# First phase of a fused mixer and expert kernel: shift and scale in two halves, with the input loaded first

## The chip, the core and the metric

The kernel runs as one program on one core of one Trainium2 chip. The metric is the device time of one execution in microseconds, 1215.98 us as the median of three runs (1215.55 to 1216.28). TensorE (PE in the profile) multiplies, ScalarE (ACT) and VectorE (DVE) work on tiles in SBUF and PSUM, GpSimd (POOL) does a few side operations, and SyncE (SP) issues nearly all the loads.

## The reference

One layer over 512 latent tokens of width 1024, with 256 context tokens. What the change touches is the head of the layer: six modulation vectors from the conditioning, of which the first two are shift and scale, and the normalised and modulated input h, from which every projection is made.

```python
sc = jax.nn.silu(c); scc = jax.nn.silu(c_ctx)
mod = jnp.split(sc @ w_ada[layer] + b_ada[layer], 6, axis=-1)
mod_c = jnp.split(scc @ w_ada[layer] + b_ada[layer], 6, axis=-1)
h = _modulate(_rmsnorm(x, norm1_w[layer]), mod[0][:, None], mod[1][:, None])    # h * (1 + scale) + shift
hc = _modulate(_rmsnorm(xc, norm1_w[layer]), mod_c[0], mod_c[1])
q, k, v, z, xbc, dtr, fu, su = _split_in(h @ w_in)
...    # four mixers: window attention, SSD, 2-D DFT, gated convolution
out = _merge(h, branches, w_gate, b_gate, w_branch, w_o)
x = x + mod[2] * out
h2 = _modulate(_rmsnorm(x, norm2_w[layer]), mod[3], mod[4])
x = x + mod[5] * _moe(h2, w_router, router_bias, w1, w3, w2)
return _rmsnorm(x, final_norm_w)
```

## The kernel before

Activations lie transposed: Hx holds x as 8 blocks (KD = 8) of 128 channels by 512 tokens. Each block is normalised, scaled by A1 = (1 + scale) * norm weight, and shifted. For the projections a block is split in two rounded parts, Hhi (ScalarE) and Hlo (VectorE), and a weight tile in ring_hi and ring_lo; a projection adds three products, hi by hi, hi by Hlo and lo by Hhi. The V projection instead uses the whole Hx with WV, four products of 144 columns per block, one for each 128 tokens.

The work is one list of steps, `timeline()`, written by hand. TensorE, ScalarE, VectorE and GpSimd each go through this list in its order and do their part of each step; `tile_order()` derives from it the order in which the tiles of the weight stream are loaded. An engine never overtakes in its own part. Semaphores join the engines; `full[b]` says that PSUM bank b is written, `empty[b]` that it is read.

The steps of the first phase are these. `("mr", u)`: the product of the two silu vectors with unit u of w_ada (a 512-column piece of 2048 KB; units 0 and 1 hold the shift, units 2 and 3 the scale), eight products into a PSUM bank that ScalarE copies to `modrow[u]`. `to_columns(u)`: four products of two columns each that turn that row into columns. `("ssq",)`: the sum of squares of x over the partitions, from which ScalarE's root and VectorE's reciprocal make `rsx`. `("mod", 0)`: VectorE adds the bias to shift and scale (`mods`), makes A1, and the eight blocks are modulated and split. `("csq",)`, `("ssqc",)`: the same sums for the context. `("xbc", 0)`: the first projection tile and, woven into it, the V products; `("v", c)` only carries its results. `keep_warm(n)` is n products of ones, whose result nobody reads. Modulation row and block: unit 0 gives the shift of blocks 1 to 4, unit 2 their scale, units 1 and 3 those of blocks 5 to 8.

SyncE issues the loads at the program's start in the order cols, rows, ada 0, ada 1, x, ada 2, ada 3, and then the stream of tiles, with WV behind the first one and the context behind the second.

Of the kernel before, what the change touches and what calls it, by code (L numbers as in the profile page):

```python
# [26 lines left out]
P = 128  # L27
# [159 lines left out]
def bank_plan(steps):  # L187
# [3 lines left out]
    for s in steps:  # L191
# [26 lines left out]
        elif k in ("ssq", "ssqc"):  # L218
            b = 3
        elif k in ("ynorm", "macc", "zk", "rtk", "dt", "csq"):  # L220
            continue
        elif k in ("mr", "v"):
            b = 4 + s[1]
        elif k == "z":
            b = 3 + s[1]
        elif k == "rt":
            b = 7
        elif k == "g2":
            b = 3
        elif k == "pick":  # L230
            b = s[1]
        elif k == "bexp":
            b = 5
        elif k == "up0":
            continue
        else:
            b = 7
# [54 lines left out]
def build(nc, xT, ctxT, adaw, stream, consts, cossin, dft, cols, rows, wv, wrt, umap, wa, wb, w2, h2d, ybuf, gfin, out):  # L292
# [12 lines left out]
    ada = [at(f"ada{i}", o, [P, UNIT]) for i, o in enumerate((32768, 73728, 90112, 177344))]  # L305
# [160 lines left out]
    hm_ready, h_ready, padz = map(sem, "hm_ready h_ready padz".split())  # L466
# [103 lines left out]
    def _(sp):  # L570
        sp.dma_start(QC[:, :], cols).then_inc(small_in, 16)
        sp.dma_start(RW[:, :], rows).then_inc(small_in, 16)
        sp.dma_start(ada[0][:, :], adaw[0]).then_inc(ada_in[0], 16)
        sp.dma_start(ada[1][:, :], adaw[1]).then_inc(ada_in[1], 16)
        sp.dma_start(Hx[:, :, :], xT).then_inc(x_in, 16)
        sp.dma_start(ada[2][:, :], adaw[2]).then_inc(ada_in[2], 16)
        sp.dma_start(ada[3][:, :], adaw[3]).then_inc(ada_in[3], 16)
        rings = {True: [], False: []}
        for i, x in enumerate(order):
# [22 lines left out]
            if x == ("xbc", 0):  # L602
                sp.dma_start(WV[:, :, :], wv).then_inc(wv_in, 16)
            if x == ("xbc", 1):
                sp.dma_start(hcx[:, :, :], ctxT).then_inc(c_in, 16)
# [72 lines left out]
    def _(pe):  # L678
# [65 lines left out]
        def to_columns(u):  # L744

            job_read(pe, ("mr", u))
            for j in range(4):
                o = (4 * u + j) * 2
                ins = mm(bk(0)[:, o:o + 2], modrow[:, u, j * P:j * P + P], QC[:, Q_SUM:Q_SUM + 2], True, True)
# [6 lines left out]
        def project(s, cols, x, ctx_side):  # L756
# [7 lines left out]
            return ins.then_inc(full[b], 1)  # L764

        for s in steps:
# [17 lines left out]
            elif k0 == "mr":  # L784
# [5 lines left out]
                if u > 1:  # L790
                    for q in ((0, 1), (2,))[u - 2]:
                        to_columns(q)
                    if u == 2:
                        keep_warm(8)
# [5 lines left out]
            elif k0 == "mod":  # L800
                to_columns(3).then_inc(full[0], 1)
            elif s == ("xbc", 0):

                b, hi, lo = claim(pe, s), hi_place(s), lo_place(s)
                keep_warm(3)
                for c in range(NCH):
                    claim(pe, ("v", c))
                pe.wait_ge(hi_ready, 1)
                for k in range(KD + 1):
                    if k < KD:  # L810
                        w = hi[:, k * P:k * P + P]
                        pe.wait_ge(hhi_ready, k + 1)
                        mm(bk(b), w, Hhi[:, k, :], k == 0, False)
                        pe.wait_ge(hlo_ready, k + 1)
                        mm(bk(b), w, Hlo[:, k, :], False, False)
                    if k:
                        if k == 1:
                            pe.wait_ge(wv_in, 16)
                        pe.wait_ge(h_ready, k)
                        for c in range(NCH):  # L820
                            ins = mm(bk(4 + c)[:, 0:VD], Hx[:, k - 1, c * P:c * P + P], WV[:, k - 1, :], k == 1, k == KD)
                            if k == KD:
                                ins.then_inc(full[4 + c], 1)
                pe.wait_ge(lo_ready, 1)
                for k in range(KD):
                    ins = mm(bk(b), lo[:, k * P:k * P + P], Hhi[:, k, :], False, k == KD - 1)
                ins.then_inc(full[b], 1)
# [332 lines left out]
    def _(act):  # L1160
# [16 lines left out]
        for s in steps:  # L1177
# [16 lines left out]
            elif k0 == "mr":  # L1194
                b, _n = plan[s]
                if s[1] == 2:
# [6 lines left out]
                if s[1] == 3:  # L1203
                    split_hi(0)
            elif s == ("mod", 0):

                def whole(k):
                    act.wait_ge(hlo_ready, k + 1)
                    A(Hx[:, k, :], Hx[:, k, :], ACT.Identity, bias=mods[:, k, 0:1]).then_inc(*t(h_ready))

                for k in range(KD):
                    act.wait_ge(hm_ready, k + 1)
                    A(Hhi[:, k, :], Hx[:, k, :], ACT.Identity, bias=mods[:, k, 0:1]).then_inc(*t(hhi_ready))
                    if k:
                        whole(k - 1)
                whole(KD - 1)
                split_hi(1)
            elif k0 == "csq":
                act.wait_ge(c_in, 16)
                for k in range(NCC * 2):  # L1220
                    A(sq[:, KD + k, :], hcx[:, 2 * k:2 * k + 2, :].rearrange("p a n -> p (a n)"), ACT.Square).then_inc(*t(sq_ready))
            elif k0 in ("xbc", "xbcc"):
# [223 lines left out]
    def _(v):  # L1446
# [95 lines left out]

        sum_squares(0, KD)

        for s in steps:
# [5 lines left out]
            if k0 in ("ssq", "ssqc", "ssq2"):  # L1551
# [3 lines left out]
                else:  # L1555
                    out = {"ssq": rsx, "ssqc": rsc}[k0]
                    link(V_.reciprocal(out[:, :], out[:, :]))
                    if k0 == "ssqc":
# [7 lines left out]
            elif k0 == "csq":  # L1566
                sum_squares(KD, KD + NCH)
            elif k0 == "sw":
                job_full(v, s)
                V_.tensor_copy(swv[:, :], bk(b)[:, 0:NE]).then_inc(*t(empty[b], plan[s][1]))  # L1570
            elif s == ("mod", 0):
                job_full(v, s)
                TT(mods[:, 0:16, :], bk(b)[:, 0:32].rearrange("p (j w) -> p j w", w=2),
                   hb(QC[:, Q_BADA:Q_BADA + 16], 2), ALU.add).then_inc(*t(empty[b], plan[s][1]))
# [702 lines left out]
```

## Time and profile before

| | |
|---|---|
| median of three runs | 1215.98 us |
| profiled execution | 1215.87 us |
| its span | 1214.0 us |
| TensorE busy | 1130.3 us (93%) |
| VectorE busy | 558.7 us (46%) |
| ScalarE busy | 315.0 us (26%) |
| GpSimd busy | 127.1 us (10%) |
| mean granted TensorE clock | 0.985 |
| moved by DMA | 273.87 MB, mean 226 GB/s |

The span runs from the first to the last recorded instruction, and the execution's own time is 1.9 us more. Times in the rows count from the span's start. A row of the timeline gives start, duration, engine and line, the operation with what it writes and reads, how many instructions are merged in it, and in brackets how long the engine was idle before and what it waited for. One fp32 product of TensorE stands as two instructions, so eight products appear as x16.

### The profile page before, as it was taken

The page shows a single profiled execution, that of the slowest core. Times are in us where ns is not written, and L with a number is a line of the kernel's source. Part 1 is how long each engine was busy: PE and PEld are TensorE (multiplying, and loading weights), DVE is VectorE, ACT ScalarE, POOL GpSimd, SP SyncE. Part 2 cuts the span into 40 slices and gives each one's busy share as a digit, 9 for nine tenths or more (in the row PEclk, how much of TensorE's full clock was granted, in tenths as well). Part 3 has the DMA queues.
Part 4 walks back from the last instruction along what each step waited for, and adds up shares of the span by engine and source line. Part 5 has one row for each costly group of instructions (what it writes and reads, how often), then busy time and mean ns, then how long its engine had stood idle before and what let it go on. Part 6 is the DMA issues. An engine that isn't in the chain of part 4 may idle for free.

```text
span 1214.0 us, 16058 instructions
## 1 busy us (share of the span) xinstructions
PE 1130.3 (93%) x5708; PEld 708.7 (58%) x5708; DVE 558.7 (46%) x987; ACT 315.0 (26%) x537; POOL 127.1 (10%) x180
## 2 busy tenths in 40 slices
PE   4999999999999999999999999899999999977786
PEld 2788878877666777777778787433333333322223
DVE  2777577735676776656454455421112111211114
ACT  3653312133333434323333333100000000000003
POOL 0000000000120010012000100122112222211110
PEclk8899999999999999999999998999999999999998
DMA  9422636620111111112212567899999999999965
GB/s 386 163 87 93 255 138 227 236 93 18 53 53 53 53 53 52 53 52 86 71 64 93 195 247 275 353 403 388 418 426 426 420 426 413 425 428 424 426 280 218
DMA packets 39573, 273.87 MB, mean 226 GB/s; under 512 B 7274, under 2 KB 7786, under 8 KB 27616
## 3 DMA queue, kind: packets, MB, share of 16 engines
q1 hardware_dynamic: 33920, 264.89, 54.3%
q0 software_dynamic: 5600, 8.26, 1.9%
q8 instruction: 34, 0.56, 0.2%
q14 instruction: 19, 0.16, 0.0%
HBM read 269.86 MB, written 13.37 MB: 233 GB/s over the span
## 4 chain that ended last, share of the span: by engine, by line
PE 75%; DMA 11%; DVE 8%; ACT 3%; issue 2%; SPq 1%; DVEq 0%; POOL 0%; ACTq 0%; POOLq 0%
PE psum L680 71%; DMA ering<-in_wb 9%; DMA ada<-in_adaw 2%; DVE amx L1712 1%; DVE sc L1701 1%; PE psum L696 1%; PE psum L982 1%; DMA xr<-token_rows,tabt 1%; DVE ring_lo L1456 1%; PE psum L718 1%; DVE ytmp L1456 1%; ACT ring_hi L1163 1%; ACT E L1163 0%; DVE sg L1456 0%; PE psum L1063 0%
## 5 line engine op out<-in xcount | busy, mean ns | idle before, releaser
L680 PE MATMUL psum<-ering,xs 128*64 128x512 f32 x1056 | 237.3, 600 | 27.3 <-DMA ering<-in_wb 14.4
L680 PE MATMUL psum<-Hhi,ring_hi 128*128 128x512 f32 x472 | 192.8, 408 | 2.7 <-DVE ring_lo L1456 1.7
L680 PE MATMUL psum<-Hlo,ring_hi 128*128 128x512 f32 x472 | 186.3, 395 | 0.1
L680 PE MATMUL psum<-Hhi,ring_lo 128*128 128x512 f32 x472 | 182.9, 390 | 0.0
L680 PEld LDWEIGHTS psum<-ering,xs 128*64 128x64 f32 x1056 | 72.8, 137 | 168.9 <-issue 132.3
L1456 DVE TENSOR_TENSOR ring_lo<-ring,ring_hi 128x1024 fp32r<-128x1024 f32 x83 | 102.9, 1239 | 104.6 <-ACT ring_hi L1163 103.3
L1456 DVE TENSOR_TENSOR sg<-sg,psum 128x256 f32<-128x256 f32 x66 | 27.8, 421 | 259.2 <-ACT sg L1163 258.0
L680 PE MATMUL psum<-ering,at 128*64 128x512 f32 x528 | 119.4, 597 | 0.7 <-DVE ysb L1456 0.7
L1163 ACT ACTIVATE ring_hi<-ring 128x1024 fp32r<-128x1024 f32 x83 | 88.0, 1060 | 78.3 <-DMA ring<-in_stream 49.9
L680 PEld LDWEIGHTS psum<-Hhi,ring_hi 128*128 128x128 f32 x472 | 89.2, 189 | 26.8 <-issue 8.6
L680 PEld LDWEIGHTS psum<-Hlo,ring_hi 128*128 128x128 f32 x472 | 89.1, 189 | 20.9 <-issue 2.4
L680 PEld LDWEIGHTS psum<-Hhi,ring_lo 128*128 128x128 f32 x472 | 88.5, 188 | 19.9
L1163 ACT ACTIVATE sg<-psum 128x256 f32<-128x256 f32 x33 | 12.7, 383 | 243.2 <-PE psum L680 243.1
L680 PEld LDWEIGHTS psum<-ering,at 128*64 128x64 f32 x528 | 35.5, 136 | 65.2 <-issue 65.2
L1456 DVE TENSOR_TENSOR ysb<-psum,G 128x512 f32<-128x512 f32 x33 | 22.8, 691 | 80.3 <-PE psum L680 77.0
L1163 ACT ACTIVATE gth<-psum,half 128x512 f32<-128x512 f32 x32 | 22.0, 688 | 124.2 <-PE psum L680 119.3
L1163 ACT ACTIVATE at<-psum 128x256 f32<-128x256 f32 x33 | 12.7, 383 | 141.1 <-PE psum L718 141.1
L2058 POOL TENSOR_TENSOR xdd<-xs,wdd 128x512 f32<-128x512 f32 x10 | 10.4, 1042 | 331.2 <-DVE zs L1684 241.0
L680 PE MATMUL psum<-bhi,ring_hi 128*128 128x512 f32 x96 | 40.9, 426 | 0.0
L1163 ACT ACTIVATE sc<-sc,amx 128x512 f32<-128x512 f32 (+1 forms) x32 | 24.8, 776 | 56.0 <-DVE amx L1713 56.0
L680 PE MATMUL psum<-blo,ring_hi 128*128 128x512 f32 x96 | 38.0, 395 | 0.0
L680 PE MATMUL psum<-bhi,ring_lo 128*128 128x512 f32 x96 | 38.0, 395 | 0.0
(339 smaller groups left out, 1525.8 us busy)
## 6 DMA issues: line engine op xcount, KB each, us to landing
ering<-in_w SPq DMA_DIRECT2D x28, 2048.0 KB, 16.1
ering<-in_wb SPq DMA_DIRECT2D x28, 2048.0 KB, 18.3
ering<-in_wa SPq DMA_DIRECT2D x28, 2048.0 KB, 16.6
ring<-in_stream SPq DMA_DIRECT2D x87, 512.0 KB, 4.1
ada_ring<-in_stream SPq DMA_DIRECT2D x32, 512.0 KB, 3.6
ada<-in_adaw SPq DMA_DIRECT2D x4, 2048.0 KB, 16.9
gat<-expert_rows SPq DMA_DIRECT2D x4, 1024.0 KB, 8.3
Hx<-in_xT SPq DMA_DIRECT2D x1, 2048.0 KB, 16.9
```

The lines of the kernel that those rows point to most:

```text
L680: return nc.tensor.matmul(out, lhsT, rhs, start=start, stop=stop)
L696: ins = nc.tensor.transpose(XT[h][:, q * P:q * P + P], xr[h][:, q * P:q * P + P], ID)
L718: ins = nc.tensor.transpose(AT[h][:, q * P:q * P + P], sg[h][:, q * P:q * P + P], ID)
L982: ins = nc.tensor.transpose(bk(b, 2)[:, i * P:i * P + P], sc[:, h % 3, i * P:i * P + P], ID)
L1163: return nc.scalar.activation(out, in_, f, **kw)
L1456: return V_.tensor_tensor(out, a, b, op)
L1701: ins = V_.scalar_tensor_tensor(sc[:, h % 3, 0:S], bk(3 + g), HD ** -0.5, CT[:, C_MASK + mo:C_MASK + mo + S], ALU.mult, ALU.add)
L1712: link(V_.tensor_reduce(amx[:, h, 0:1], sc[:, h % 3, 0:W], AX.X, ALU.max))
L2058: G_.tensor_tensor(xdd[:, :].rearrange("p (h n) -> p h n", h=8), xs[:, c, :].rearrange("p (h n) -> p h n", h=8), hb(wdd[:, c, d * 8:d * 8 ...
```

## The change

The list of steps is written anew at its head. Only units 0 and 2 are multiplied before `("mod", 0)`, which now makes shift, scale and A1 of blocks 1 to 4 alone. `("xa", 0)` and `("xa", 1)` hold the first four blocks' products of the first tile and of V, with `("mr", 1)` between them; `("mr", 3)` and the new `("modb",)` make the second half, and `("xbc", 0)` keeps blocks 5 to 8. The loads go out as x, ada 0, ada 2, first tile, WV, ada 1, ada 3, context. The modulation itself is rewritten: VectorE multiplies a block by rsx alone, ScalarE makes Hhi from that with A1 as scale and the shift as bias, VectorE makes the whole block with both, and subtracts Hhi for Hlo; ScalarE's second pass over Hx is gone. The sixteen warming products stand ahead of the first unit, eight before unit 2, and the three before the first tile are gone. Four of the first tile's eight lo products come before the last two-column products.

```diff
-    t = [("mr", 0), ("mr", 1), ("mr", 2), ("ssq",), ("mr", 3), ("mod", 0), ("csq",), ("xbc", 0)] + [("v", c) for c in range(NCH)]
+    t = [("mr", 0), ("ssq",), ("mr", 2), ("mod", 0), ("xa", 0), ("mr", 1), ("xa", 1), ("mr", 3), ("modb",), ("csq",), ("xbc", 0)]
+    t += [("v", c) for c in range(NCH)]
...
+        sp.dma_start(Hx[:, :, :], xT).then_inc(x_in, 16)
         sp.dma_start(ada[0][:, :], adaw[0]).then_inc(ada_in[0], 16)
-        sp.dma_start(ada[1][:, :], adaw[1]).then_inc(ada_in[1], 16)
-        sp.dma_start(Hx[:, :, :], xT).then_inc(x_in, 16)
         sp.dma_start(ada[2][:, :], adaw[2]).then_inc(ada_in[2], 16)
-        sp.dma_start(ada[3][:, :], adaw[3]).then_inc(ada_in[3], 16)
...
             if x == ("xbc", 0):
                 sp.dma_start(WV[:, :, :], wv).then_inc(wv_in, 16)
+                sp.dma_start(ada[1][:, :], adaw[1]).then_inc(ada_in[1], 16)
+                sp.dma_start(ada[3][:, :], adaw[3]).then_inc(ada_in[3], 16)
+                sp.dma_start(hcx[:, :, :], ctxT).then_inc(c_in, 16)
...                                                              (TensorE)
+        def first_blocks(k):
+            x = ("xbc", 0)
+            b, w = plan[x][0], hi_place(x)[:, k * P:k * P + P]
+            pe.wait_ge(hhi_ready, k + 1)
+            mm(bk(b), w, Hhi[:, k, :], k == 0, False)
+            pe.wait_ge(hlo_ready, k + 1)
+            mm(bk(b), w, Hlo[:, k, :], False, False)
...
+                    pe.wait_ge(x_in, 16)
+                    keep_warm(16)
+                if u == 2:
+                    to_columns(0)
+                    keep_warm(8)
+                if u == 3:
+                    claim(pe, ("modb",))
+                    to_columns(1)
...
+            elif k0 == "modb":
+                pe.wait_ge(lo_ready, 1)
+                for k in range(4):
+                    lo_block(k)
+                to_columns(3).then_inc(full[3], 1)
+            elif k0 == "xa":
...
+                for k in range(2 * s[1], 2 * s[1] + 2):
+                    first_blocks(k)
+                    if k:
+                        v_blocks(k - 1)
+                if s[1] == 1:
+                    v_blocks(3)
...                                                              (ScalarE)
+            elif k0 == "modb" or s == ("mod", 0):
+                act.wait_ge(a1_ready, 1 + (k0 == "modb"))
+                for k in range(4) if k0 == "mod" else range(4, KD):
                     act.wait_ge(hm_ready, k + 1)
-                    A(Hhi[:, k, :], Hx[:, k, :], ACT.Identity, bias=mods[:, k, 0:1]).then_inc(*t(hhi_ready))
+                    A(Hhi[:, k, :], Hx[:, k, :], ACT.Identity, scale=A1[:, k, 0:1], bias=mods[:, k, 0:1]).then_inc(*t(hhi_ready))
...                                                              (VectorE)
+        def over_root(k):
+            TT(Hx[:, k, :], Hx[:, k, :], rsx[:, :], ALU.mult).then_inc(*t(hm_ready))
...
+                for k in range(o, o + 4):
+                    if k < 3:
+                        over_root(k + 1)
                     v.wait_ge(hhi_ready, k + 1)
+                    V_.tensor_scalar(Hx[:, k, :], Hx[:, k, :], A1[:, k, 0:1], mods[:, k, 0:1], ALU.mult, ALU.add).then_inc(*t(h_ready))
+                    v.wait_ge(h_ready, k + 1)
+                    TT(Hlo[:, k, :], Hx[:, k, :], Hhi[:, k, :].bitcast(F32), ALU.subtract).then_inc(*t(hlo_ready))
+                if k0 == "mod":
+                    split_lo(0)
+                    for k in range(4, KD):
+                        over_root(k)
```

On TensorE, the program's head before the change, up to the products of block 3 (ada_54 to ada_57 are units 0 to 3, one_t the warming products, `psum<-QC,modrow` the two-column products, WV,Hx a V group):

```order
L680 MATMUL psum<-ada_54,silp 32x512 x8
L680 MATMUL psum<-ada_55,silp 32x512 x8
L680 MATMUL psum<-QC,modrow 128x2 x8
L680 MATMUL psum<-one_t 128x128 x8
L680 MATMUL psum<-ada_56,silp 32x512 x8
L680 MATMUL psum<-sq,one_t 128x512
L680 MATMUL psum<-QC,modrow 128x2 x4
L680 MATMUL psum<-ada_57,silp 32x512 x8
L680 MATMUL psum<-QC,modrow 128x2 x4
L680 MATMUL psum<-one_t 128x128 x3
L680 MATMUL psum<-Hhi,ring_hi 128x512
L680 MATMUL psum<-Hlo,ring_hi 128x512
```

The same engine in the changed kernel, from the last two-column products before the first block to those of the last unit:

```order
L683 MATMUL psum<-QC,modrow 128x2 x4
L683 MATMUL psum<-Hhi,ring_hi 128x512
L683 MATMUL psum<-Hlo,ring_hi 128x512
L683 MATMUL psum<-Hhi,ring_hi 128x512
L683 MATMUL psum<-Hlo,ring_hi 128x512
L683 MATMUL psum<-WV,Hx 128x144 x4
L683 MATMUL psum<-ada_55,silp 32x512 x8
L683 MATMUL psum<-Hhi,ring_hi 128x512
L683 MATMUL psum<-Hlo,ring_hi 128x512
L683 MATMUL psum<-WV,Hx 128x144 x4
L683 MATMUL psum<-Hhi,ring_hi 128x512
L683 MATMUL psum<-Hlo,ring_hi 128x512
L683 MATMUL psum<-WV,Hx 128x144 x8
L683 MATMUL psum<-QC,modrow 128x2 x4
L683 MATMUL psum<-ada_57,silp 32x512 x8
L683 MATMUL psum<-Hhi,ring_lo 128x512 x4
L683 MATMUL psum<-QC,modrow 128x2 x4
```

Units 1 and 3 stood ahead of every product of a block; now unit 1 has two blocks and one V group ahead of it, and unit 3 four blocks and four V groups.

On VectorE, the changed kernel from the first A1 on (before, each block had two SCALAR_TENSOR_TENSOR, one for Hx and one for Hlo):

```order
L1608 SCALAR_TENSOR_TENSOR A_116<-mods,QC 128x8
L1479 TENSOR_TENSOR Hx<-Hx,rsx 128x512
L1615 TENSOR_SCALAR Hx<-Hx,A_116,mods 128x512
L1479 TENSOR_TENSOR Hlo<-Hx,Hhi 128x512
L1479 TENSOR_TENSOR Hx<-Hx,rsx 128x512
L1615 TENSOR_SCALAR Hx<-Hx,A_116,mods 128x512
L1479 TENSOR_TENSOR Hlo<-Hx,Hhi 128x512
```

A block of the first half has three operations in a row there, one of the second half two, since its product with rsx is done before the second A1.

## Rows read from the trace of the kernel before

**Rows 1.** Chain of waits, 0 to 70 us: start, duration, what.
```profile
3.05 21.27 DMA ada<-in_adaw
...
24.37 8.26 PE psum L680 x42
...
38.70 15.20 PE psum L680 x85
```

**Rows 2.** Load issues: timeline, ada tiles' landing times, and the page's issue list.
```profile
1.64 0.42 SPq L573 DMA_DIRECT2D ada<-in_adaw  x1
...
2.58 0.43 SPq L575 DMA_DIRECT2D Hx<-in_xT  x1
...
3.60 0.76 SPq L577 DMA_DIRECT2D ada<-in_adaw  x1
...
DMA to landing us min/median/max: 8.0/16.9/25.6
...
Hx<-in_xT SPq DMA_DIRECT2D x1, 2048.0 KB, 16.9
```

**Rows 3.** Timeline of TensorE, 9 to 33 us.
```profile
9.78 3.33 PE L680 MATMUL psum<-ada,silp 128*32 128x512 f32 x16 [9.78 <-DMA ada<-in_adaw]
...
14.58 1.92 PE L680 MATMUL psum<-ada,silp 128*32 128x512 f32 x16 [1.46 <-DMA ada<-in_adaw]
...
16.43 1.95 PE L680 MATMUL psum<-QC,modrow 128*128 128x2 f32 x16
...
18.24 2.03 PE L680 MATMUL psum<-one_t 128*128 128x128 f32 x16
...
24.37 3.64 PE L680 MATMUL psum<-ada,silp 128*32 128x512 f32 x16 [4.10 <-DMA ada<-in_adaw]
...
27.94 2.01 PE L680 MATMUL psum<-sq,one_t 128*128 128x512 f32 x2
...
30.66 1.92 PE L680 MATMUL psum<-ada,silp 128*32 128x512 f32 x16
```

**Rows 4.** Timeline, 33 to 35 us: last two-column products, bias, A1.
```profile
33.37 1.05 PE L680 MATMUL psum<-QC,modrow 128*128 128x2 f32 x8 [0.78 <-ACT modrow L1163]
34.53 0.19 DVE L1456 TENSOR_TENSOR mods<-psum,QC 128x32 f32<-128x32 f32 x1 [0.34 <-PE psum L680]
34.75 0.18 DVE L1576 SCALAR_TENSOR_TENSOR A<-mods,QC 128x16 f32<-128x16 f32 x1
```

**Rows 5.** Windows of 1 us: engines' busy time, then granted clock, DMA share, GB/s.
```profile
22.00:23.00 1.00, 0.00 (x0) 0.00 (x0) 0.93 (x3) 1.00 (x3) 0.00 (x0) 0.96 1.11 475
29.00:30.00 1.00, 1.00 (x5) 0.51 (x3) 0.00 (x0) 0.00 (x0) 0.00 (x0) 0.63 1.05 422
36.00:37.00 1.00, 0.32 (x1) 0.28 (x1) 0.81 (x2) 1.00 (x2) 0.00 (x0) 0.79 1.06 438
43.00:44.00 1.00, 1.00 (x7) 0.96 (x7) 1.00 (x3) 1.00 (x3) 0.00 (x0) 0.80 0.03 12
```

**Rows 6.** Groups by form: busy us, mean ns of one, idle before.
```profile
L1456 DVE TENSOR_TENSOR sq<-sq 128x512 f32<-128x512 f32 x10 | 6.9, 692 | 16.0 <-ACT sq L1163 15.6
...
L1602 DVE TENSOR_SCALAR macc<-ada_ring,sil 128x512 f32<-128x512 f32 x8 | 3.9, 486 | 7.3 <-DMA ada_ring<-in_stream 7.1
...
L1557 DVE RECIPROCAL rsx<-rsx 128x512 f32<-128x512 f32 x1 | 3.4, 3352 | 5.0 <-ACT rsx L1163 5.0
...
L1163 ACT ACTIVATE Hhi<-Hx,mods 128x512 fp32r<-128x512 f32 x8 | 5.7, 720 | 1.6 <-DVE Hx L1579 1.6
...
L1163 ACT ACTIVATE sq<-Hx 128x512 f32<-128x512 f32 x8 | 4.3, 614 | 2.3 <-DMA Hx<-in_xT 2.3
```

**Rows 7.** Timeline of TensorE: V groups at both clocks, eight lo products.
```profile
39.29 2.12 PE L680 MATMUL psum<-WV,Hx 128*128 128x144 f32 x8
...
44.16 1.14 PE L680 MATMUL psum<-WV,Hx 128*128 128x144 f32 x8
...
51.79 2.10 PE L680 MATMUL psum<-Hhi,ring_lo 128*128 128x512 f32 x8
```

**Rows 8.** Timeline: the copy of the first tile's result, and the first context tile.
```profile
54.01 0.60 ACT L1163 ACTIVATE pads<-psum 128x512 f32<-128x512 f32 x1 [2.83 <-PE psum L680]
...
66.44 0.36 PE L680 MATMUL psum<-hchi,ring_hi 128*128 128x256 f32 x1 [0.69 <-DVE hclo L1456]
```

More of the change, by code:

```diff
@@ L217, in bank_plan @@
             b = 0
-        elif k in ("ssq", "ssqc"):
+        elif k in ("ssq", "ssqc", "modb"):
             b = 3
-        elif k in ("ynorm", "macc", "zk", "rtk", "dt", "csq"):
+        elif k == "mr" and s[1] % 2:
+            b = 1 + s[1] // 2
+        elif k in ("ynorm", "macc", "zk", "rtk", "dt", "csq", "xa"):
             continue
@@ L304, in build @@
     Hlo = at("Hlo", 177344, [P, KD, S], FR)
-    ada = [at(f"ada{i}", o, [P, UNIT]) for i, o in enumerate((32768, 73728, 90112, 177344))]
+    ada = [at(f"ada{i}", o, [P, UNIT]) for i, o in enumerate((32768, 73728, 177344, 90112))]
     modrow = at("modrow", 110784, [P, 4, S])
@@ L764, in project, with lo_block, v_blocks @@
             return ins.then_inc(full[b], 1)
+        def first_blocks(k):
[5 more added lines that the diff above has]
+            mm(bk(b), w, Hlo[:, k, :], False, False)
+        def lo_block(k):
+            x = ("xbc", 0)
+            return mm(bk(plan[x][0]), lo_place(x)[:, k * P:k * P + P], Hhi[:, k, :], False, k == KD - 1)
+        def v_blocks(k):
+            pe.wait_ge(h_ready, k + 1)
+            for c in range(NCH):
+                ins = mm(bk(4 + c)[:, 0:VD], Hx[:, k, c * P:c * P + P], WV[:, k, :], k == 0, k == KD - 1)
+                if k == KD - 1:
+                    ins.then_inc(full[4 + c], 1)
         for s in steps:
@@ L800, in _ @@
             elif k0 == "mod":
-                to_columns(3).then_inc(full[0], 1)
-            elif s == ("xbc", 0):
[L804 to L827, printed above, removed]
@@ new lines, in _ @@
+                to_columns(2).then_inc(full[0], 1)
+            elif k0 == "modb":
[4 more added lines that the diff above has]
+            elif k0 == "xa":
+                if s[1] == 0:
+                    claim(pe, ("xbc", 0))
+                    for c in range(NCH):
+                        claim(pe, ("v", c))
+                    pe.wait_ge(hi_ready, 1)
+                    pe.wait_ge(wv_in, 16)
+                for k in range(2 * s[1], 2 * s[1] + 2):
[4 more added lines that the diff above has]
+                    v_blocks(3)
+            elif s == ("xbc", 0):
+                for k in range(4, KD):
+                    first_blocks(k)
+                    if k > 4:
+                        v_blocks(k - 1)
+                v_blocks(KD - 1)
+                for k in range(4, KD):
+                    ins = lo_block(k)
+                ins.then_inc(full[plan[s][0]], 1)
@@ L1591, in _ @@
+                if k0 == "mod":
+                    split_lo(0)
+                    for k in range(4, KD):
+                        over_root(k)
             elif k0 == "macc":
```

54 lines of the change are left out of this document (18 added, 36 removed).

## Prediction

> **What bounds the kernel now.** The change touches only the first 54 us, so I read the chain of waits of that stretch first. It shows one DMA wait of 21.27 us up to 24.3 us, then TensorE for 8.26 us, and from 38.70 us TensorE again for 15.20 us, to 53.9 us [rows 1]. That last moment, when the first projection tile (xbc 0) and the V products are complete, is the yardstick below: all later work follows it. Next the DMA issues: the loads are queued one behind another, and each 2048 KB load lands about 4.9 us after the one ahead: ada 0 at 9.6 us, Hx at 19.5, the last at 29.2 (issue plus time to landing), the others evenly between [rows 2]. Unit 3 of w_ada, the second half of the scale, lands at 29.2 us, but its products start at 30.66 [rows 3]: TensorE is late for its own load by 1.5 us. A1 is ready at 34.93 us [rows 4]. Last the granted clock. It falls from full (2.4 GHz) to half (1.2 GHz) late in the slice 22 to 23 us, after TensorE has stood idle since 20.3, and again in 36 to 37 us, after a stretch with only the two-column products and the three warming products; it is back in 29 to 30 us, 5.0 us after dense work began at 24.37, and in 43 to 44 us, 6.7 us after 36.7 [rows 5]. At 9.78 us the column shows full speed, but eight products take 3.33 us there and 1.92 us later [rows 3], so the first burst runs at about half speed too.
>
> **Loads.** Hx now stands where ada 0 stood and lands at 9.6 us, ada 0 at 14.5, ada 2 at 19.5. Behind them come the ring tile and WV (512 and 576 KB, at 4.9 us for 2048 KB together 2.6 us: 22.1), ada 1 (27.0) and ada 3 (31.9), 2.7 us later than now.
>
> **Up to the first A1.** The sixteen warming products start at 9.75. Eight cost 2.03 us at full speed [rows 3], 0.254 each. The bounds are 4.1 us (full throughout, hidden before the load at 14.5) and 8.1 us (half throughout, end at 17.9). I take half speed for the first 3.3 us, as the first burst has it now: 6.5 products, the other 9.5 cost 2.4 us, end 15.45. Products of unit 0: 1.92, to 17.4; the sum product, 2.01 at half speed [rows 3], 1.0 here, to 18.4; its inputs are there (eight squares of 0.61 with additions of 0.69 behind them [rows 6], 16 us). Two-column products of unit 0: 1.0, eight warming products 2.03, to 21.4; unit 2: 1.92, to 23.3. Copy and hand-over 0.72, four two-column products 1.05 [rows 4], three small VectorE operations instead of two (0.51 plus 0.2 [rows 4]): A1 of blocks 1 to 4 at 25.8 us, 9.1 us earlier than now. The reciprocal, 3.35 us [rows 6], started at about 19.1 and is done.
>
> **First half, blocks 1 to 4.** ScalarE's Hhi has a scale read from a tensor besides the bias. A tensor bias costs 0.11 us (0.720 against 0.614 for the squares [rows 6]); no row has both operands. Between 0.72 and 0.94 I take 0.82. The Trainium skill, "ScalarE: Activation LUTs", section "What ACT_TABLE_LOAD costs", gives each such pointer operand about 93 ns; the trace's 106 for one agrees, and by the page the two places where this Hhi heads a chain cost 0.19 us together. VectorE has three operations per block instead of two: Hx times rsx (0.69), the TENSOR_SCALAR (0.49, as the macc row) and the subtraction (0.69) [rows 6], with hand-overs 1.95 us. Hlo of block 1 stands at 27.8, of 2 at 29.75, of 3 at 31.7, of 4 at 32.95. Dropping ScalarE's second pass over Hx gains nothing, ScalarE being free here.
>
> **What now stands between the scale's second half and TensorE.** TensorE takes instructions in written order. ada 1 and ada 3 wait behind products: the V group of block 1 ahead of unit 1, then blocks 3 and 4 with three more V groups, the two-column products of unit 1, and only then unit 3. From 30.0 us, at full speed: four V groups at 1.14 (4.56), units 1 and 3 (3.84), four Hhi/Hlo products at 0.23 (2.10 for eight, less the tail of the last; 0.92) [rows 7], two-column products 1.0, four lo products 0.92 (they cover the copy of unit 3's result), two-column products 1.05: 12.3 us, so 42.3. The load of ada 3, landed at 31.9, is met only near 40: it isn't the bound any more. But the clock. From 23.3 to 30.0 TensorE has four two-column products and three 512-column ones, less than before either fall now. I take the clock as half from there and back 5.0 us after 30.0 (the burst at 24.37 is dense like this one; 6.7 is the other bound). A V group takes 2.12 at half against 1.14 [rows 7], so 5.0 us at half lose 2.3. Ready at 44.6. The skill's rule against this change, "TensorE: Matmul & The Clock Gate", section "HAM oscillation — how this bites in real kernels", says in my words that each wait long enough drops the clock and makes the next burst begin slow; the rows of both falls agree. By that rule both gaps pay; by a clock that holds, neither.
>
> **Second half, blocks 5 to 8.** Small operations 0.75: A1 at 45.4. Hhi 0.82, TENSOR_SCALAR and Hlo 1.23: 47.5; each further Hlo 1.25 later (Hx times rsx was done beside the first half, by 37), so that of block 6 at 48.75. Until then TensorE has had three products since 44.6, again a gap of 4 us. From 48.8: one Hlo product 0.23, four V groups 4.56, two more blocks 0.92, four lo products 0.92: 6.6, to 55.4. The clock again costs 2.3: 57.7 us against 53.9. So +3.8 us.
>
> Nothing gives it back later. The context chain starts from this same end; at 66.44 us TensorE has been idle 0.69 us for it [rows 8], which is all that a slow start of the next tile could hide. Csq, the context squares and the splits of ring tiles 2 and 3 lie beside the V products as now. The DMA queue is idle after 43 us [rows 5], so the moved loads delay none. GpSimd's clearing of pads waits for unit 1's products and moves to about 35 us, long before the first copy into pads [rows 8]. The profiled execution took 1215.87 us (span 1214.0 plus 1.9 around it), 0.1 under the median of 1215.98: 1215.87 + 3.8 = 1219.7 us.
>
> **Rivals.**
>
> A. The clock holds. Sixteen warming products lie at the head and V products in the first gap's wake; if neither gap drops the clock both terms of 2.3 go: 53.1, and if the warming products run at full speed too, unit 0 starts 0.85 earlier: 52.3, so -1.6 us, 1214.3. It decides at xbc 0's end: not slower from 53.9 down, which needs nearly both gaps. For it: two-column and warming products kept the clock between 16.4 and 20.3. Against: both falls now followed lighter work of 3 to 4 us.
>
> B. One gap keeps the clock, or falls only after it, so that one term stays: +1.5, 1217.4.
>
> C. The warming products run at half speed throughout, end at 17.9 (+2.4), and unit 0 follows at half (3.64 against 1.92, +1.7): 1223.8. For it: no row shows what 128-column products alone do to a clock that is down. Against: the eight 512-column products restored it by 14.58.
>
> D. The products of unit 3 meet their load, as its early place in the queue suggests. From 31.9: unit 3 1.92, copy 0.72, columns 1.05, small operations 0.75, second A1 at 36.3; Hlo of block 6 3.3 us later, then 6.6 and 2.3: 48.6, so -5.3, 1210.6. For it: now unit 3 does follow its load by 1.5 us only. Against: the written order puts 8.4 us of other products between 30.0 and unit 3, so this needs my reading of who waits for whom to be wrong.
>
> **Chances.** Forecast 0.50, with its own range 1218.3 to 1222.0 (the second bound of the clock's return, 6.7 instead of 5.0 us, twice 0.8, and Hhi's price). A 0.13, B 0.17, C 0.15, D 0.05. What a measurement here can tell from no change is 0.2%, 2.4 us: the edges are 1213.5 and 1218.4. Slower: nearly all of the forecast and C, 0.64. Same: A, B and the forecast's fringe, 0.27. Faster: D and a part of A, 0.09. The range of 8 in 10 takes in A and nearly C: 1214.0 to 1223.5.
>
> **What would show it.** Right: A1 of the first half near 26 us, a granted clock that falls in 24 to 29 us and again around 45 to 49, unit 1's products after 31 us although ada 1 landed at 27, unit 3's near 40, the second A1 near 45, and pads of xbc 0 near 57.8 instead of 54.01 [rows 8]. Wrong: full clock across either gap, unit 3 before 36 us, or VectorE's blocks at another pace than 1.95 and 1.25 us. From the tile after xbc 0 on, every row should stand at one constant distance from its place now.

## The result, and the profile after

| | before | after |
|---|---|---|
| median, 7 runs of each side by side | 1215.98 us (1214.49 to 1219.37) | 1220.41 us (1219.57 to 1221.75) |
| ratio to before, 95% interval | | 1.0032 (1.0019 to 1.0045) |
| profiled execution | 1215.87 us | 1221.74 us |
| its span | 1214.0 us | 1219.9 us |
| mean granted TensorE clock | 0.985 | 0.979 |

The medians lie 4.4 us apart, and the ratio makes it 3.9 us (2.3 to 5.5); 3.8 us were forecast. One execution of before beside a later experiment took 2891.94 us and is left out of its ratio. The chain of waits of the changed kernel, 0 to 60 us (start, duration, what), answers to [rows 1]:

```profile
1.64 8.15 DMA Hx<-in_xT
...
9.92 13.82 PE psum L683 x90
...
24.48 0.90 PE psum L683 x7
25.38 0.79 issue
26.16 0.82 ACT Hhi L1193
...
30.12 14.65 PE psum L683 x89
...
45.39 0.82 ACT Hhi L1193
...
46.31 0.56 DVE Hx L1615
...
46.89 0.70 DVE Hlo L1479
...
47.64 9.35 PE psum L683 x43
```

The long load wait is gone from the chain: x, at its start, is the only load in it. In its place the chain leaves TensorE twice for several microseconds, at 25.4 and at 44.8 us, for the small operations, ScalarE and VectorE. The 14.65 us on TensorE between them are the stretch in which unit 3 is queued behind products. TensorE's timeline (start, duration, instructions merged, idle before) answers to [rows 3, 7]:

```profile
9.92 6.34 PE L683 MATMUL psum<-one_t 128*128 128x128 f32 x32 [9.92 <-DMA Hx<-in_xT]
...
16.19 1.92 PE L683 MATMUL psum<-ada,silp 128*32 128x512 f32 x16
...
24.48 1.05 PE L683 MATMUL psum<-QC,modrow 128*128 128x2 f32 x8 [0.78 <-ACT modrow L1193]
...
30.71 2.12 PE L683 MATMUL psum<-WV,Hx 128*128 128x144 f32 x8
...
32.77 3.35 PE L683 MATMUL psum<-ada,silp 128*32 128x512 f32 x16
...
36.63 1.14 PE L683 MATMUL psum<-WV,Hx 128*128 128x144 f32 x8
...
40.91 1.92 PE L683 MATMUL psum<-ada,silp 128*32 128x512 f32 x16
...
49.41 2.12 PE L683 MATMUL psum<-WV,Hx 128*128 128x144 f32 x8
```

The first V group, unit 1 and the V group at 49.41 run at half speed, the V group at 36.63 and unit 3 at full. The same in windows of one us (each engine's busy time, then granted clock, DMA share, GB/s), as in [rows 5]:

```profile
28.00:29.00 1.00, 0.67 (x2) 0.30 (x2) 1.00 (x3) 0.08 (x1) 0.00 (x0) 0.94 0.96 410
...
35.00:36.00 1.00, 1.00 (x8) 0.00 (x0) 1.00 (x2) 0.00 (x0) 0.00 (x0) 0.65 1.00 418
...
45.00:46.00 1.00, 0.00 (x0) 0.00 (x0) 0.27 (x3) 0.61 (x1) 0.00 (x0) 0.97 0.00 0
...
52.00:53.00 1.00, 1.00 (x6) 0.90 (x6) 0.97 (x2) 0.58 (x1) 0.00 (x0) 0.61 0.08 25
```

The clock falls from full (2.4 GHz) to half (1.2 GHz) at the end of 28 to 29 us and of 45 to 46 us, each time in a stretch in which TensorE mostly waits, and comes back in 35 to 36 and 52 to 53. The yardstick, against 54.01 us in [rows 8]:

```profile
57.09 0.60 ACT L1193 ACTIVATE pads<-psum 128x512 f32<-128x512 f32 x1 [4.51 <-PE psum L683]
```

### The profile page after: what moved, and what is told of

Its sections match the earlier page's. It is cut to its first block, busy times and chain, and to the rows that moved or that the text cites. A ratio compares the mean times of both kernels' runs of the same rounds, so it can differ in the third digit from the quotient of the medians.

```text
span 1219.9 us, 16117 instructions
## 1 busy us (share of the span) xinstructions
PE 1141.6 (94%) x5734; PEld 716.9 (59%) x5734; DVE 562.2 (46%) x999; ACT 310.3 (25%) x529; POOL 127.1 (10%) x180
## 4 chain that ended last, share of the span: by engine, by line
PE 76%; DMA 10%; DVE 8%; ACT 3%; issue 2%; SPq 0%; DVEq 0%; POOL 0%; ACTq 0%; POOLq 0%
PE psum L683 73%; DMA ering<-in_wb 6%; DMA ering<-in_wa 3%; DVE amx L1743 1%; DVE sc L1732 1%; PE psum L699 1%; PE psum L1012 1%; DMA xr<-token_rows,tabt 1%; DVE ring_lo L1479 1%; PE psum L721 1%; DMA Hx<-in_xT 1%; DVE ytmp L1479 1%; ACT ring_hi L1193 1%; ACT E L1193 0%; DVE sg L1479 0%
## 5 line engine op out<-in xcount | busy, mean ns | idle before, releaser
L683 PE MATMUL psum<-ering,xs 128*64 128x512 f32 x1056 | 240.7, 607 | 23.6 <-DMA ering<-in_wa 11.8
```

The lines of the kernel that those rows point to most:

```text
L683: return nc.tensor.matmul(out, lhsT, rhs, start=start, stop=stop)
```

## The experiments

The theory: the loss is the order of TensorE's work. Unit 3 waits behind products instead of for its load, and each of the two gaps costs its waiting and then time at half clock. The rivals: the gaps' clock is worth nothing; the modulation's extra VectorE work carries the loss; unit 3 is load-bound. Below, "copy" is the start of the copy into pads, after at 57.09 and before at 54.01 us. Each ratio is to runs of before on the same chip, with its 95% interval; the medians of before there were 1217.5 to 1217.6 us, not 1215.98, so the ratios say more than the medians. The copy also carries what happened before the change's order matters: the first half's two-column products (unit 2's) come at 23.6 to 24.7 us, as the head's warming products take 5.6 to 6.6 us. Where it matters, the stretch from those products to the copy is given, 57.09 - 24.48 = 32.61 us in the changed kernel (32.49 in its second profile).

**Second gap filled by order.** `e1_units_first`:

```diff
-    ("mod", 0), ("xa", 0), ("mr", 1), ("xa", 1), ("mr", 3), ("modb",), ("csq",), ("xbc", 0)]
+    ("mod", 0), ("xa", 0), ("mr", 1), ("mr", 3), ("modb",), ("xa", 1), ("csq",), ("xbc", 0)]
```

> The changed kernel with units 1 and 3 and the second A1 moved ahead of blocks 3 and 4 and their V groups (steps xa 0, mr 1, mr 3, modb, xa 1). Theory (TensorE's written order makes the second A1 late, and the gap it leaves costs the clock): A1 comes at about 42.5 us instead of 45.3, blocks 3 and 4 fill the gap of 44.8 to 47.6, the granted clock does not fall there, and the copy into pads stands at about 53.5 us instead of 57.09: about 3.5 us under the changed kernel, level with before (-0.5 to +1). Rival (the second half waits for loads or for VectorE's pace, not for TensorE's order): pads stays at 56 to 57 and the time within 1 us of the changed kernel.

Measured: 1214.20 us (7 runs), ratio 0.9963 (0.9949 to 0.9976). Its timeline:

```profile
40.80 0.95 PE L683 MATMUL psum<-QC,modrow 128*128 128x2 f32 x8
...
52.54 0.60 ACT L1193 ACTIVATE pads<-psum 128x512 f32<-128x512 f32 x1 [2.96 <-PE psum L683]
```

The copy comes 4.55 us earlier than in the changed kernel, and the stretch is 28.16 us, 4.45 less. Only two blocks' products moved: they now fill the second gap, and the granted clock stays at 1.00 through 44 to 48 us. The rival that the order behind unit 1 is indifferent is out.

**Second gap filled with warming products alone.** `e4_warm_second_gap`, in the modb step of TensorE:

```diff
                 to_columns(3).then_inc(full[3], 1)
+                keep_warm(11)
```

> The changed kernel with eleven warming products (2.8 us at full speed) behind the last two-column products, that is in the gap of 44.8 to 47.6 us. They add no wait, since Hlo of block 5 is not there before 47.6. Theory (the second gap's price is the clock, 2 to 2.5 us): the granted clock stays at 1.00 from 36 us on, pads stands at about 54.8 instead of 57.09, -2.3 us. Rival (the clock falls all the same, because such products don't count as work, or TensorE waits for VectorE's blocks anyway): pads within 0.5 us of 57.09, time unchanged.

Measured: 1216.22 us (12 runs), ratio 0.9988 (0.9977 to 0.9999). Its timeline:

```profile
24.74 1.05 PE L683 MATMUL psum<-QC,modrow 128*128 128x2 f32 x8 [0.78 <-ACT modrow L1194]
...
45.00 2.70 PE L683 MATMUL psum<-one_t 128*128 128x128 f32 x22
...
55.60 0.60 ACT L1194 ACTIVATE pads<-psum 128x512 f32<-128x512 f32 x1 [2.63 <-PE psum L683]
```

The gap's wait is still there, only its clock is kept: no fall from 37 us to the copy. From unit 2's two-column products to the copy the changed kernel takes 57.09 - 24.48 = 32.61 us, this one 30.86. So the second gap's clock alone is worth 1.75 us (1.9 if counted from the second A1 on), and the rest of what the order gave, 2.7 us, is the waiting itself.

**Both gaps.** `e5_warm_both_gaps`, in addition:

```diff
                 to_columns(2).then_inc(full[0], 1)
+                keep_warm(6)
...
                     first_blocks(k)
+                    if k == 0:
+                        keep_warm(5)
```

> The changed kernel with eleven warming products in the second gap, where they kept the clock full and brought the copy into pads from 57.09 to 55.60, and now also six behind the first half's two-column products and five behind the first Hlo product, in the gap of 25.4 to 30.1 us. Theory (the first gap costs about 2.3 us by its clock): the clock does not fall near 29 us, unit 1's products take 1.9 us instead of 3.4, pads at 53 to 53.7. Rival (such products do not keep the clock here, or they delay the first block): the fall stays, pads at 55.5 or later.

Measured: 1214.45 us (12 runs), ratio 0.9983 (0.9971 to 0.9995). Its timeline, and its windows in the two gaps:

```profile
24.12 1.05 PE L683 MATMUL psum<-QC,modrow 128*128 128x2 f32 x8 [0.78 <-ACT modrow L1197]
...
31.18 1.92 PE L683 MATMUL psum<-ada,silp 128*32 128x512 f32 x16
...
52.17 0.60 ACT L1197 ACTIVATE pads<-psum 128x512 f32<-128x512 f32 x1 [2.64 <-PE psum L683]
```

```profile
28.00:29.00 1.00, 1.00 (x8) 0.96 (x9) 0.99 (x2) 0.44 (x1) 0.00 (x0) 1.00 1.11 475
...
45.00:46.00 1.00, 0.54 (x3) 0.23 (x2) 0.97 (x2) 0.97 (x3) 0.00 (x0) 1.00 0.00 0
```

The clock is full across both, and unit 1 takes 1.92 instead of 3.35 us. The same stretch takes 52.17 - 24.12 = 28.05 us: the first gap's clock is worth 30.86 - 28.05 = 2.81 us. Both together 4.56; forecast twice 2.3. Each price rests on one profile, but the stretch itself came out within 0.12 us in the two profiles of the changed kernel.

**Unit 1 before every block.** `e2_unit1_before_blocks`:

```diff
-    ("mod", 0), ("xa", 0), ("mr", 1), ("xa", 1), ("mr", 3), ("modb",), ("csq",), ("xbc", 0)]
+    ("mod", 0), ("mr", 1), ("xa", 0), ("mr", 3), ("modb",), ("xa", 1), ("csq",), ("xbc", 0)]
```

> The changed kernel with units 1 and 3 even earlier: steps mod 0, mr 1, xa 0, mr 3, modb, xa 1, so that unit 1 is multiplied when its load lands (27.0) and unit 3 after the first V group alone. Theory (written order): unit 3's products at about 33 us, second A1 at 37.6, blocks 3 and 4 fill the wait for block 5; with full clock throughout the copy into pads comes at 48.7, with one fall of the clock at up to 51, against 52.54 with the order xa 0, mr 1, mr 3, modb, xa 1; about 2 to 4 us under that kernel. Rival (VectorE's three operations per block, or the copy of unit 1's result behind four Hhi, now set the pace): pads at 51.5 or later, gain under 1 us.

Measured: 1213.09 us (9 runs), ratio 0.9961 (0.9947 to 0.9975). Its timeline:

```profile
28.11 3.25 PE L683 MATMUL psum<-ada,silp 128*32 128x512 f32 x16 [3.41 <-DMA ada<-in_adaw]
...
34.18 1.92 PE L683 MATMUL psum<-ada,silp 128*32 128x512 f32 x16
...
48.80 0.60 ACT L1193 ACTIVATE pads<-psum 128x512 f32<-128x512 f32 x1 [2.95 <-PE psum L683]
```

Unit 1 starts when its load has landed, unit 3 at 34.18 instead of 40.91, and the copy is 8.3 us earlier than in the changed kernel. Of that 0.8 us is the head's own scatter; the stretch is 48.80 - 23.65 = 25.15 us, 7.5 less. With the same halves and loads the copy is now 5.2 us ahead of before's: the queueing was the loss, not the split.

**Blocks' products with rsx taken out of the first half.** `e3_roots_ahead`, on top of that:

```diff
                     if k0 == "ssq":
-                        over_root(0)
+                        for k in range(4):
+                            over_root(k)
...
-                    if k < 3:
-                        over_root(k + 1)
```

> As the kernel with units 1 and 3 earliest (mod 0, mr 1, xa 0, mr 3, modb, xa 1), and VectorE multiplies blocks 1 to 4 by rsx before the first A1, in the 1.5 us in which it waits there now, instead of one per block between. Theory: a block's pace goes from 1.8 to 1.2 us, Hhi of block 4 is done at about 29.4 instead of 31.5 and so the copy of unit 1's result, unit 3's products meet their load at 31.9; copy into pads another 1.2 us earlier than in that kernel, 47.5 to 50. Rival (VectorE is not what unit 3 waits for): no difference beyond 0.3 us.

Measured: 1211.96 us (8 runs), ratio 0.9958 (0.9945 to 0.9972), against 0.9961 for the one above on the same chip. The copy is at 48.66 against 48.80. The rival held: in this order VectorE's three operations per block aren't the limit of the head. Unit 3 starts at 34.04, behind a unit 1 that still runs at half clock (27.84, for 3.40 us).

**The same with the gap before unit 1 warmed.** `e6_ahead_and_warm`:

```diff
                 to_columns(2).then_inc(full[0], 1)
+                keep_warm(9)
```

> As the kernel with unit 1 first and VectorE's four products by rsx ahead (copy into pads at 48.66, 1211.96 us), with nine warming products (2.3 us) behind the two-column products of unit 2, in the 3.2 us in which TensorE waits for unit 1's load. Theory (unit 1's products take 3.40 us there only because the clock is half): no fall of the clock in the first 60 us, unit 1 1.92 us, unit 3's products start with their load near 32 instead of 34.04, copy into pads at 47.0 to 47.6, 1 to 2 us less. Rival (the second A1 is then bound by the load of ada 3 and the gain stops at 0.5 us, or the warming products delay unit 1): copy at 48.2 or later.

Measured: 1210.71 us (1207.64 to 1212.32, 6 runs), ratio 0.9936 (0.9917 to 0.9954). Its timeline:

```profile
25.38 2.25 PE L683 MATMUL psum<-one_t 128*128 128x128 f32 x18
...
28.00 1.92 PE L683 MATMUL psum<-ada,silp 128*32 128x512 f32 x16 [0.37 <-DMA ada<-in_adaw]
...
32.89 1.92 PE L683 MATMUL psum<-ada,silp 128*32 128x512 f32 x16
...
47.51 0.60 ACT L1194 ACTIVATE pads<-psum 128x512 f32<-128x512 f32 x1 [2.96 <-PE psum L683]
```

The granted clock is 1.00 up to the copy, and unit 3's products now start with their load. The stretch is 47.51 - 24.46 = 23.05 us, 2.0 less than without the nine products. This is the version that beats both kernels, by 7.8 us against before and, by the ratios, by 11 to 12 against the changed kernel. It keeps the changed kernel's loads, halves and modulation; only the order of the steps, nine warming products and the place of four VectorE products differ.

**The modulation alone.** `e7_modulation_alone`: the kernel before with its order, loads and warming products, and only the new operations of VectorE and ScalarE:

```diff
...                                                              (ScalarE)
-                    A(Hhi[:, k, :], Hx[:, k, :], ACT.Identity, bias=mods[:, k, 0:1]).then_inc(*t(hhi_ready))
-                    if k:
-                        whole(k - 1)
...
+                    A(Hhi[:, k, :], Hx[:, k, :], ACT.Identity, scale=A1[:, k, 0:1], bias=mods[:, k, 0:1]).then_inc(*t(hhi_ready))
...                                                              (VectorE)
-                        scaled(k + 1)
+                        over_root(k + 1)
...
-                    V_.scalar_tensor_tensor(Hlo[:, k, :], Hx[:, k, :], mods[:, k, 0:1], Hhi[:, k, :].bitcast(F32), ALU.add,
-                                            ALU.subtract).then_inc(*t(hlo_ready))
+                    V_.tensor_scalar(Hx[:, k, :], Hx[:, k, :], A1[:, k, 0:1], mods[:, k, 0:1], ALU.mult, ALU.add).then_inc(*t(h_ready))
+                    v.wait_ge(h_ready, k + 1)
+                    TT(Hlo[:, k, :], Hx[:, k, :], Hhi[:, k, :].bitcast(F32), ALU.subtract).then_inc(*t(hlo_ready))
```

> The kernel before with only the change's modulation: VectorE multiplies by rsx, TENSOR_SCALAR and subtraction, ScalarE's Hhi with scale and bias; order of steps and loads as before. Theory (three VectorE operations per block, 1.8 us, against 1.33): Hlo of block 8 at about 50 instead of 46.1, with two V groups and eight lo products behind it: copy into pads at 55 to 55.5 instead of 54.01, +1 to +1.5 us. Rival (TensorE, at half clock for its first blocks and 1.44 us per block later, hides it): copy within 0.4 us of 54.01.

Measured: 1216.29 us (11 runs), ratio 0.9993 (0.9981 to 1.0005): no difference. Its timeline:

```profile
32.22 1.05 PE L680 MATMUL psum<-QC,modrow 128*128 128x2 f32 x8 [0.78 <-ACT modrow L1163]
...
47.62 0.69 DVE L1450 TENSOR_TENSOR Hlo<-Hx,Hhi 128x512 fp32r<-128x512 f32 x1
...
53.24 0.60 ACT L1163 ACTIVATE pads<-psum 128x512 f32<-128x512 f32 x1 [2.19 <-PE psum L680]
```

From the two-column products to the copy it takes 21.02 us, before 54.01 - 33.37 = 20.64 [rows 4, 8] (20.60 and 20.75 in its two later profiles): the new modulation costs 0.3 to 0.4 us there, though the last Hlo comes about 3 us later behind its A1. The rival held: TensorE, with V groups between the blocks, hides it. That holds for the order of before. In the changed kernel's first gap TensorE does wait for VectorE (30.12 us, for block 2's Hlo), and what the extra operation costs there was not run by itself.

**The head's warming products left out.** `e8_no_head_warming`:

```diff
-                    pe.wait_ge(x_in, 16)
-                    keep_warm(16)
```

> The changed kernel without the sixteen warming products and the wait for x at its head. Unit 0's products then start with their load, 14.5 us, instead of 16.19. Theory (the warming products end 1.7 us after that load and so cost what they save): unit 0's products take 3.3 us as the first burst of before, end at 17.9 instead of 18.1, and the time is within 0.5 us of the changed kernel. Rival (they save a half-speed start of 3 us or more, since without them the clock stays half through unit 0, the sum product and unit 2): first A1 at 27.5 or later instead of 26.1, +1.5 to +3 us.

Measured: 1224.34 us (6 runs), ratio 1.0050 (1.0036 to 1.0064). Its timeline:

```profile
14.54 3.64 PE L683 MATMUL psum<-ada,silp 128*32 128x512 f32 x16 [14.54 <-DMA ada<-in_adaw]
...
24.54 1.05 PE L683 MATMUL psum<-QC,modrow 128*128 128x2 f32 x8 [0.78 <-ACT modrow L1191]
...
56.59 0.60 ACT L1191 ACTIVATE pads<-psum 128x512 f32<-128x512 f32 x1 [4.26 <-PE psum L683]
```

The sixteen products buy little before the first A1: unit 0 starts 1.65 us earlier, at half clock, and the two-column products come at 24.54, against 23.57 to 24.74 in the eight profiles with them. The second fall comes late here, at the end of 48 to 49 us, when TensorE has work again. In the head, then, the theory held, but the ratio is 2.2 us over the changed kernel's, which the intervals don't clearly part. The trace has two falls more, far behind the head, in windows whose clock is 1.00 in both profiles of the changed kernel:

```profile
792.00:804.00 12.00, 9.59 (x40) 3.63 (x42) 1.98 (x3) 0.38 (x1) 3.65 (x6) 0.86 1.01 424
...
1146.00:1158.00 12.00, 9.89 (x40) 3.09 (x38) 1.08 (x3) 0.39 (x1) 0.60 (x2) 0.86 1.02 428
```

Behind the first one the distance to before's rows has gone from +6.2 to +8.1 us and stays there; the second leaves no such mark. What brings the falls there stays open.

**A delay given to before.** `e9_before_plus_3us`: does the later program simply follow the head?

```diff
+                if k0 == "ssqc":
+                    keep_warm(12)
```

> The kernel before with twelve warming products (3.05 us at full speed) between the first tile and the context's sum product: all behind it is moved by the amount by which the change moved it, and nothing else. In the changed kernel's profile the distance to before is 3.1 us from 57 to 260 us but 5.9 at the end, with additional falls of the clock near 268, 545 and 1098 us. Theory (those are chance of the single execution): +3.0 us in the median (0.25%), with other places and numbers of late clock falls. Rival (a shift of 3 us lines the later waits up badly with the clock's observation, every time): +5 to +6 us and falls at the same places.

Measured: 1215.75 us (12 runs), ratio 0.9980 (0.9971 to 0.9989). Its timeline:

```profile
14.41 3.64 PE L680 MATMUL psum<-ada,silp 128*32 128x512 f32 x16 [1.16 <-DMA ada<-in_adaw]
...
24.20 2.93 PE L680 MATMUL psum<-ada,silp 128*32 128x512 f32 x16 [2.31 <-DMA ada<-in_adaw]
...
52.50 2.84 PE L680 MATMUL psum<-one_t 128*128 128x128 f32 x24
52.77 0.60 ACT L1165 ACTIVATE pads<-psum 128x512 f32<-128x512 f32 x1 [2.73 <-PE psum L680]
```

Neither theory held. The warming products took 2.84 us, and the kernel was 2.4 us faster. Part of it is the head, 1.24 us earlier in this profile though its code there is that of before. Unit 1's products, at 14.41, still ran at half speed (3.64 us, 1.92 in [rows 3]); so TensorE was idle for 2.31 us and not 4.10 before unit 2, and the clock fell at about 25 us and not at 22.9 [rows 5], and was back in 28 to 29 and not in 29 to 30. About 1 us of the delay did not arrive: the distance to before's rows goes from -1.2 us at the copy to +0.6 at 70 us, 1.8 for 2.84. For the rest, the late falls lie elsewhere: before's at 288 to 294 us is missing (-1.0 from 303 us on), one at 540 to 546 us is new (+0.5), and the end stands at -1.1. The experiment shows that a delay isn't passed on one to one; what moves the late falls it doesn't show.

**The changed kernel and the kernel before, once more.** `after_again` is the changed kernel unaltered, `before_again_1` and `before_again_2` the kernel before:

> The changed kernel once more, unchanged. In its first profile the copy into pads is 3.1 us later than before, and falls of the clock near 268, 545, 1098 and 1128 us that before's profile does not have make it 5.9 us at the end; six timed kernels of this case spread by 1 to 5 us over their runs. Theory (the head's 3 us is the change's own; the late falls come and go with the execution): copy into pads at 55.5 to 58.5, ratio to before within 1.001 to 1.004, and late falls in part at other places. Rival (the late falls belong to this kernel): the same four places again, ratio 1.004 or more.

> The kernel before, unchanged, for a second profile. Its timed runs spread from 1214.6 to 1220.6 us, so one profile is one draw. Theory (late falls of the clock come and go with the execution): falls at other places than near 290, 740 and 1160 us, and a copy into pads between 52.7 and 55 us, depending on when the head's two falls come. Rival (they belong to the kernel): the same three places, and a time within 0.5 us of 1215.9.

> A third profile of the kernel before. Theory: if this one's time is 2 us or more from the first profile's 1215.87, the difference lies in the number of late falls, 1 to 2 us each, and in the head's falls, not in any wait of another kind. Rival: the difference lies in the loads of the expert phase, with the same falls.

Measured: 1220.65 us (9 runs), ratio 1.0029 (1.0014 to 1.0043), copy at 56.48; and 1215.24 and 1215.99 us, one run each, copy at 53.83 and 54.19. Windows of the changed kernel in the first profile, then of before in its first, in two stretches far behind the change:

```profile
264.00:270.00 6.00, 5.16 (x26) 3.95 (x25) 0.17 (x1) 2.03 (x4) 0.00 (x0) 0.82 0.00 0
...
546.00:552.00 6.00, 6.00 (x17) 4.67 (x17) 0.00 (x0) 0.00 (x0) 0.00 (x0) 0.57 0.00 0
```

```profile
264.00:270.00 6.00, 6.00 (x30) 5.32 (x31) 0.17 (x1) 2.05 (x2) 0.00 (x0) 1.00 0.00 0
...
546.00:552.00 6.00, 6.00 (x22) 3.77 (x21) 3.92 (x5) 3.74 (x5) 1.04 (x1) 1.00 0.22 74
```

Both profiles of the changed kernel show these two falls (after_again has 0.76 and 0.63 in these windows), none of the three of before does: there both windows have 1.00. (Before's own fall at 288 to 294 us, 0.72, is in the changed kernel too, at 294 to 300.) These two are repeatable, not noise of one execution. Two more of the first profile (1098 to 1104 us at 0.78, 1128 to 1134 at 0.72) are not: after_again has 1.00 there. Likewise before has its falls near 290 and 740 us in all three profiles, but those from 1086 us on differ from one to the next. So of the theories in both expectations half held: some late falls belong to the kernel, some to the execution.

## Why the prediction came out as it did

Where the difference lies, by place. It is the distance of the same rows of the profiles, after minus before; the profiles lie 5.9 and 5.3 us apart, more than the medians:

| place | first profile of after | after_again |
|---|---|---|
| copy into pads (54 us) | +3.1 | +2.5 |
| 266 to 326 us | +4.3 to +4.8 | +3.7 to +4.1 |
| 546 us | +7.7 | +7.1 |
| 743 to 790 us | +6.8 to +6.2 | +6.2 to +5.5 |
| end | +5.8 to +5.9 | +5.2 to +5.3 |

So 2.5 to 3.1 us come from the head, as the theory says, and the rest of the profiles' difference, some 2.8 us net, from where the clock falls later: the two extra falls cost 1.7 and 3.1 us, and some 1.5 come back between 740 and 800 us, where before's fall is the longer one. How far the head and the whole agree, over all kernels (the stretch from unit 2's two-column products to the copy, in kernels with the changed head; copy minus 54.01; ratio less one, times the median of before):

| kernel | stretch, us | copy, us | whole, us |
|---|---|---|---|
| after | 32.6 | +3.1 | +3.9 |
| e8, no head warming | 32.1 | +2.6 | +6.1 |
| e4, second gap warm | 30.9 | +1.6 | -1.5 |
| e7, modulation alone | | -0.8 | -0.9 |
| e9, before with a delay | | -1.2 | -2.4 |
| e1, units first | 28.2 | -1.5 | -4.5 |
| e5, both gaps warm | 28.1 | -1.8 | -2.1 |
| e2, unit 1 ahead | 25.2 | -5.2 | -4.7 |
| e3, roots ahead | 25.1 | -5.4 | -5.1 |
| e6, ahead and warm | 23.1 | -6.5 | -7.8 |

The whole follows the head, with up to 3.5 us either way on top. The changed kernel's 3.9 to 4.4 us, at 2.5 to 3.1 in the head, are thus no finer proof of the forecast's 3.8 than that.

Step by step:

- **Who waits for whom.** Right. Unit 1 started at 32.77 and unit 3 at 40.91 (forecast "near 40"), and rival D is out. The loads were in, though each about 1 us later than forecast: unit 3's landed at 33.0 instead of 31.9, and unit 1's at about 28 instead of 27, by the runs that wait for it (28.11 in e2, 28.00 in e6). e1 and e2 show it by experiment: with the order undone the stretch is 4.5 and 7.5 us shorter.
- **The clock in the gaps.** Right. Falls at the end of 28 to 29 and of 45 to 46 us, price 2.8 and 1.75 us against 2.3 each; their sum is as forecast, which is in part luck. The 5.0 us was misread from [rows 5]: a clock of 0.63 in 29 to 30 us puts the return at 29.7, 5.4 us behind 24.37. Here the clock stayed at half for 5.6 us behind 30.12, and the first gap cost more. Behind the second gap, TensorE at full clock (e4) still waited for VectorE, 0.45 us for block 6's Hlo at 49.20, so that the first products at half cost little. Rivals A and B are out. The rule cited from the Trainium skill, "TensorE: Matmul & The Clock Gate", section "HAM oscillation — how this bites in real kernels", agrees in what follows a gap: both bursts began at half speed. The single waits that it speaks of are not what the trace shows, since both gaps were broken up by single products, and the longest wait was 1.59 us.
- **The head's warming products.** The size was off: 6.34 us for the sixteen (5.60 to 6.58 over the eight profiles that have them), so unit 0 at 16.19 instead of 15.45. Half speed held longer than the first 3.3 us that I took. It costs little at the end: first A1 at 25.91 + 0.17 = 26.08, forecast 25.8. Rival C, half throughout with unit 0 at half, is out: unit 0 took 1.92.
- **ScalarE's and VectorE's prices.** Right within 0.15 us a block. From the groups by form, changed kernel (busy us, mean ns of one, idle before), against [rows 6]:

```profile
L1193 ACT ACTIVATE Hhi<-Hx,mods,A 128x512 fp32r<-128x512 f32 x8 | 6.1, 807 | 4.8 <-DVE Hx L1479 2.2 <-DVE A L1608 1.8 <-ACT ring_hi L1193 0.8
...
L1615 DVE TENSOR_SCALAR Hx<-Hx,A,mods 128x512 f32<-128x512 f32 x8 | 4.3, 542 | 1.2 <-ACT Hhi L1193 1.2
```

  Forecast were 0.82 and 0.49. ScalarE's three forms stand at 614, 720 [rows 6] and now 807 ns for none, one and two tensor operands, 106 and 87 ns apart; the figure of the Trainium skill, "ScalarE: Activation LUTs", section "What ACT_TABLE_LOAD costs", 93 ns each, agrees within 13 ns. The blocks' pace was 1.8 and 1.18 us against 1.95 and 1.25.
- **Second half.** A1 at 45.13 + 0.17 = 45.30, forecast 45.4. Behind it 57.09 against 57.8: the lighter second price of the clock (0.55) makes most of it.
- **"At one constant distance."** Wrong. The distance goes from +3.1 to +7.7 and back to +5.8. That the sum met the median within 0.6 us is therefore partly luck; by the head alone the forecast was 0.7 us too high, by the second profile 1.3.

What stays open: why the late falls sit where they do and what moves them, and why executions of before spread over 1214.3 to 1220.6 us in the side-by-side runs while its three profiled ones lie at 1215.2 to 1216.0. With that spread the difference of one pair of profiles, +5.9, is no better a measure than the medians' +4.4.

## What to carry to other kernels

When loads are moved forward, look at the written order of the engine that uses them: a product whose load lands at 33 us but which starts 8 us later behind other work is not early, and moving it and its fellow ahead was worth 4.5 to 7.5 us at the end of the first tile. Splitting a phase in two makes a second gap on TensorE, to be charged twice, once for the wait and once for the clock behind it (1.75 and 2.8 us here); independent products put into the gap take back both, warming products only the clock. A difference of 1 to 3 us in a kernel of this length should not be read off the end of one profile; read the stretch that the change touches.

## What was not expected of the hardware

- A burst at half speed went with a faster head. In e9 and e7, whose code is that of before up to there, unit 1's products took 3.64 us instead of 1.92. That left TensorE 2.31 and 2.18 us idle before unit 2 instead of 4.10, the first fall of the clock came at about 25 us instead of 22.9, and unit 2 took 2.93 and 2.65 us instead of 3.64: both heads were some 1.1 us earlier at unit 3's two-column products. Why unit 1 ran at half speed in these two executions and not in the three of before stays open.
- Warming products of 128 columns held the clock where they filled a gap: eleven of them, 2.70 us in the second gap, kept it at 1.00, and so did nine and eleven in the first. At the head, where the clock is down, sixteen took 5.60 to 6.58 us, where eight took 2.03 at full speed [rows 3]. Whether other products would bring the clock up sooner, no run shows.
- Late falls come in two kinds. Some keep their place from execution to execution of one kernel and move with a change made hundreds of us ahead: 264 to 270 and 540 to 552 us in both profiles of after, 288 to 294 in all three of before. But a fall at 540 to 546 us is also in e4, e7 and e9, so it doesn't belong to the changed kernel alone. Others, as that at 1098 us, came in one of two executions only.
